# A single-core diffusion trunk with a 64-expert layer: a shorter routing chain, expert numbers written before the round table, the final sums moved into the last expert step, and two buffers for the split down weights

## The reference, cut to what matters

```python
h = h + g1 * mix
n2 = rmsnorm(h, lp['norm2_g']) * (1 + sc2) + sh2
h = h + g2 * moe(n2)
y = rmsnorm(h, final_norm_g)

def moe(x, lp):
    s = sigmoid(x @ w_router)                  # 64 experts in 8 groups of 8
    sel = s + b_router
    grp_score = top_k(sel by group, 2).sum(-1)
    gmask = the best 4 groups
    eidx = top 8 of where(emask, sel, NEG_BIG)
    w = s[eidx] / sum(s[eidx]) * 2.5
    y = sum over the 8 experts of w * (silu(x @ w_gate) * (x @ w_up)) @ w_down     # each 1024 -> 256 -> 1024
    return y + shared expert(x)
```

## Time and profile before

| what | value |
| --- | --- |
| median of 3 runs (lowest to highest) | 1113.5 us (1106.01 to 1113.51) |
| the profiled execution: own time, span | 1105.11 us, 1103.3 us |
| busy share of TensorE, its weight load, VectorE, ScalarE, GpSimd | 95%, 64%, 48%, 32%, 15% |
| granted TensorE clock, mean | 0.989 |
| DMA | 306.62 MB, mean 278 GB/s over the span |
| the chain that ended last, by engine | PE 60%, DVE 2%, issue 1%, ACT 1% |

### The profile page before, as it was taken

One profiled execution on the slowest core, in us unless ns is written; L12 is line 12 of the kernel. 1 busy time (PEld: TensorE's weight loads), 2 busy tenths in 40 slices (PEclk: granted clock), 3 DMA queues, 4 the chain that ended last, 5 costly groups with the idle time before them and its releaser, 6 DMA issues.

```text
span 1103.3 us, 15100 instructions
## 1 busy us (share of the span) xinstructions
PE 1046.7 (95%) x4876; PEld 702.0 (64%) x4876; DVE 531.1 (48%) x1110; ACT 355.2 (32%) x476; POOL 166.0 (15%) x142
## 2 busy tenths in 40 slices
PE   4999999999899999999998999999999999999975
PEld 2489888788788897874645455555555555454532
DVE  2233544355698956944633434433344334333358
ACT  3333544326444445501322222222222222222101
POOL 0020232000000000000015222322322212111100
PEclk9999999999999999999999999999999999999998
DMA  9999777346555332740249999999999999999692
GB/s 354 395 293 356 114 117 106 136 175 213 202 185 184 116 117 96 240 160 0 97 195 409 383 405 399 416 412 398 415 415 417 410 404 418 416 408 383 243 405 109
DMA packets 88529, 306.62 MB, mean 278 GB/s; under 512 B 13398, under 2 KB 17750, under 8 KB 66464
## 3 DMA queue, kind: packets, MB, share of 16 engines
q1 hardware_dynamic: 68896, 270.63, 62.2%
q0 software_dynamic: 12256, 26.80, 10.5%
q10 hardware_dynamic: 7328, 8.55, 2.2%
HBM read 285.31 MB, written 36.85 MB: 292 GB/s over the span
## 4 chain that ended last, share of the span: by engine, by line
PE 60%; DVE 2%; issue 1%; ACT 1%; DVEq 0%
PE PS L2045 17%; PE PS L2047 8%; PE PS L2070 4%; PE PS L1944 4%; PE PS L2031 3%; PE PS L1691 3%; PE PS L2060 3%; PE PS L2062 2%; PE PS L2061 2%; PE PS L2002 1%; PE PS L2119 1%; PE PS L2086 1%; PE PS L1932 1%; PE PS L1933 1%; PE PS L1934 1%
## 5 line engine op out<-in xcount | busy, mean ns | idle before, releaser
L1098 POOL DMA_INDIRECT y_parts<-bigB,IDX x38 | 72.3, 1902 | 323.8 <-DVE bigB L1628 314.7
L2045 PE MATMUL PS<-bigB 128*128 128x512 f32 x224 | 102.3, 600 | 0.0
L1745 PE MATMUL PS<-bigB_r 128*128 128x384 f32 x288 | 98.6, 342 | 1.3 <-ACT bigB L790 1.3
L2047 PE MATMUL PS<-bigA,bigB 128*64 128x512 f32 x208 | 94.7, 598 | 3.3 <-issue 3.3
L1747 PE MATMUL PS<-bigB_r,bigA_r 128*128 128x384 f32 x288 | 96.5, 335 | 0.0
L1746 PE MATMUL PS<-nT_r,bigB_r 128*128 128x384 f32 x288 | 96.3, 334 | 0.0
L2048 PE MATMUL PS<-bigB 128*64 128x512 f32 x208 | 94.8, 598 | 0.0
L2045 PE MATMUL PS<-bigA,bigB 128*128 128x512 f32 x208 | 94.6, 597 | 0.0
L1628 DVE TENSOR_SCALAR bigB<-PS,bigD 128x1024 f32<-128x1024 f32 x40 | 51.3, 1284 | 89.2 <-PE PS L2062 55.0
L1237 DVE TENSOR_TENSOR bigA_r<-bigA,bigB_r 128x2048 fp32r<-128x2048 f32 x18 | 41.3, 2292 | 97.5 <-ACT bigB_r L816 97.5
L1594 DVE TENSOR_TENSOR bigB<-bigB,PS 128x256 f32<-128x256 f32 x40 | 16.9, 422 | 134.3 <-ACT bigB L989 134.3
(11 more groups left out here) (372 smaller groups left out, 2127.2 us busy)
## 6 DMA issues: line engine op xcount, KB each, us to landing
bigA<-in_w_in SPq DMA_DIRECT2D x17, 2048.0 KB, 11.0
bigB<-in_w_gate SPq DMA_DIRECT2D x27, 1024.0 KB, 11.0
bigB<-in_w_up SPq DMA_DIRECT2D x27, 1024.0 KB, 18.9
bigB<-in_w_down SPq DMA_DIRECT2D x27, 1024.0 KB, 19.0
bigA<-in_w_gate SPq DMA_DIRECT2D x26, 1024.0 KB, 8.2
bigA<-in_w_up SPq DMA_DIRECT2D x26, 1024.0 KB, 16.6
bigA<-in_w_down SPq DMA_DIRECT2D x26, 1024.0 KB, 19.2
bigA<-in_w_ada SPq DMA_DIRECT2D x8, 2048.0 KB, 10.0
```

Of the source, the lines that this page charges most:

```text
L1098: pool.indirect_dma_start(y_parts, bass.IndirectOffsetOnAxis(ap=IDX[:, p, 1:2], axis=0), YS[:, p % 2, :], None, bounds_check=T * TOPK - 1, ...
L1745: mm(out, wh, nh, start=(k == 0), stop=False)
L2045: last = mm(PS[:, 2 + b, :], XT[:, b, k, :], GU_W[s][:, :, k, :], start=first, stop=stop)
L2047: mm(PS[0:HALF, 2 + b, :], XT[:, b, k, 0:HALF], GU_W[2][:, :, k, :], start=first, stop=stop)
```

## The change

It has four parts. **Routing:** the comparison of all pairs of groups is replaced by max8, match_replace and not_equal on the 8 group scores, the mask is made by one min, seven links are taken away by reordering operations that do not depend on each other, `mask_ready` is given before the weights, and the stages are in another order; the modulation of the third tile is shared between VectorE (k 0 to 3) and ScalarE (k 4 to 7), and its router product waits for one k at a time. **Numbers ahead of the table:** a new stage `row` makes the row of expert numbers before `table_t`, and SP starts its loads on it. **End inside the last step:** the final sums of VectorE and TensorE stand in the `Else` of each step (the branch of the last unit), one-hots and the first adds before the last `weigh`. **Two buffers:** `DNH` becomes a pair; `down_high` and `down_low` of a unit move one step ahead.

```diff
-          ("norm2", 2), ("rows", 0), ("route", 0), ("route", 1), ("norm_t", 2), ("rows", 1), ("sh_up", 0, 0, 2),
-          ("route", 2), ("router",), ("rows", 2), ("sh_up", 0, 2, 8), ("sh_silu", 0), ("sh_up", 1, 0, 3), ("counts",),
-          ("sh_up", 1, 3, 8), ("sh_silu", 1), ("sh_hid", 0), ("sh_hid", 1), ("sh_up", 2, 0, 3), ("table_t",),
-          ("sh_up", 2, 3, 5), ("table",), ("sh_up", 2, 5, 8), ("sh_silu", 2), ("index", 0), ("sh_down", 0), ("sh_hid", 2),
-          ("index", 1), ("sh_down", 1), ("index", 2), ("sh_down", 2), ("index", 3)]
+          ("norm2", 2), ("route", 0), ("route", 1), ("sh_up", 0, 0, 1), ("norm_t", 2), ("route", 2), ("router",),
+          ("rows", 0), ("sh_up", 0, 1, 4), ("rows", 1), ("sh_up", 0, 4, 7), ("counts",), ("rows", 2),
+          ("sh_up", 0, 7, 8), ("sh_silu", 0), ("sh_up", 1, 0, 4), ("row",), ("table_t",), ("sh_up", 1, 4, 5), ("sh_hid", 0),
+          ("table",), ("sh_up", 1, 5, 8), ("sh_silu", 1), ("index", 0), ("sh_hid", 1), ("index", 1), ("sh_up", 2, 0, 8),
+          ("sh_silu", 2), ("sh_down", 0), ("index", 2), ("sh_down", 1), ("sh_hid", 2), ("sh_down", 2), ("index", 3)]
...
-        DNH = cut(bigC_r, 0, (2, D))
+        DNH = [cut(bigC_r, 0, (2, D)), cut(bigD_r, 0, (2, D))]
...
-            units = unit_count(sp)
             sp.wait_ge(n2_out, 48)
+            sp.wait_ge(row_done, 1)
             for r, q in ((BIG0, 0), (BIG0 + 1, 1), (1, 3)):
...
+            act.wait_ge(sh_added, NT - 1)
+            down_high(1, 0)
             def step(i, p):
                 act.wait_ge(gu_ready, i)
-                if p % 3 < 2:
-                    down_high(pas * 4 + (p // 3 + 1), i, p % 3)
                 with act.If(i + 2 <= units):
                     take_xt(i + 1, p % 2)
                 act.wait_ge(ht_ready, i)
...
                 with act.If(i + 1 <= units):
+                    if (p + 1) % 3 < 2:
+                        down_high(pas * 4 + ((p + 1) // 3 + 1), (p + 1) % 3)
                     act.wait_ge(hid_done, i)
                     silu(i, (1 + p) % 2)
...
+            def last_sums():
+                dve.wait_ge(sh_added, NT)
+                one_row(0, 1, 1)
+                one_row(0, 2, 0)
+                one_row(0, 2, 1)
+                residual(0)
+                two_rows(1, 2)
+                one_row(1, 3, 0)
+                one_row(1, 3, 1)
+                final_norm(0)
+                residual(1)
+                m = 2
+                two_rows(m, 0)
+                one_row(m, 1, 0)
+                one_row(m, 1, 1)
+                link(nc.vector.tensor_tensor(ACC, ACC, gate(m), ALU.mult))
+                link(nc.vector.tensor_tensor(XH[:, m, :], XH[:, m, :], ACC, ALU.add))
+                final_norm(1)
+                dve.wait_ge(part_ready, m + 1)
+                link(nc.vector.tensor_tensor(two(ACC), PS[:, TAIL_BANK[m]:TAIL_BANK[m] + 2, :], two(gate(m)), ALU.mult))
+                nc.vector.tensor_tensor(XH[:, m, :], XH[:, m, :], ACC, ALU.add).then_inc(h2_done, 1)
+                dve.wait_ge(h2_done, m + 1)
+                final_norm(m)
...
             def step(i, p):
                 u = 1 + p + AHEAD
                 with dve.If(i + 1 <= units):
                     one_hots(pas * 8 + u // 3 * 2, u % 3, u % 2)
-                    down_low(p)
                     take_index(i + AHEAD, u % BODY, u % 3)
                     hidden_low(i, p)
+                    if (p + 1) % 3 < 2:
+                        down_low(pas * (BODY // 3 * 2) + ((p + 1) // 3 * 2 + (p + 1) % 3 + 1), (p + 1) % 3)
                     dve.wait_ge(ht_ready, i)
                     hidden(i, (1 + p) % 2)
+                    nc.vector.tensor_copy(TOKF[:, p % 2:p % 2 + 1], IDX[:, p, 0:1])
+                    weigh(i, p)
                 with dve.Else():
-                    down_low(p)
                     hidden_low(i, p)
+                    link(nc.vector.tensor_copy(TOKF[:, p % 2:p % 2 + 1], IDX[:, p, 0:1]))
+                    dve.wait_ge(ys_done, i)
+                    for b in range(2):
+                        for m in range(NT):
+                            ins = nc.vector.tensor_scalar(OHT[:, b, m, :], kc(K_R128), TOKF[:, b:b + 1], float(-P * m),
+                                                          ALU.subtract, ALU.is_equal)
+                    ins.then_inc(oht_done, 1)
+                    dve.wait_ge(xg_t, i)
+                    two_rows(0, 0)
+                    one_row(0, 1, 0)
+                    weigh(i, p)
+                    last_sums()
...
+                elif st == "row":
+                    pe.wait_ge(tab_ready, 1)
+                    mm(PS[0:1, 1, 0:RTAB], NCNT, ident, start=True, stop=True)
+                    mm(PS[0:1, 1, RTAB:2 * RTAB], RC[:, 0:1], ident, start=True, stop=True).then_inc(pr_ready, 1)
...
+            def last_sums(i):
+                pe.wait_ge(oht_done, 1)
+                pe.wait_ge(ys_done, i + 1)
+                kept_rows(0, True, False)
+                loaded_rows(0, 3, False, True).then_inc(part_ready, 1)
+                kept_rows(1, True, False)
+                loaded_rows(1, 0, False, False)
+                loaded_rows(1, 1, False, True).then_inc(part_ready, 1)
+                kept_rows(2, True, False)
+                loaded_rows(2, 2, False, False)
+                loaded_rows(2, 3, False, True).then_inc(part_ready, 1)
...
                     gate_up(i, turn, 1 + p, range(4, KD))
+                    finish_unit(i, p)
                 with pe.Else():
                     hidden_t(i, p)
-                pe.wait_ge(ht_done, i)
-                pe.wait_ge(ys_done, i)
-                down(pas * 4 + (p // 3 + 1), p)
+                    finish_unit(i, p)
+                    last_sums(i)
```

262 lines of the change are left out of this document (127 added, 135 removed).

## The result

The changed kernel takes 1153.77 us (median of 4 runs, 1147.83 to 1155.68) against 1109.97 us before (1106.01 to 1113.51): ratio 1.0387, interval 1.0325 to 1.0448. The forecast was 1115 us, its range ended at 1129. The profiled execution's span is 1151.9 us, 48.6 us more than before.

A forecast was written before the change was run, and what follows sets the result against it. TensorE's queue bounds routing, TensorE and DMA are both full in the loop, VectorE's sums bound the end. Terms 0.4 + 1 + 4 - 3.5 - 0.3 = +1.6 us on 1113.5 gave 1115 us; range 1101 to 1129.

The forecast's parts named there:

- the skipping of 8 leftover steps: End of the kernel: the skip now stands behind VectorE's last operation, 4 to 5 us against 3.1, +1 us.
- slower rival: Loop code outgrows the instruction store; fetches at three returns and the end, some +10 us, 1125 us; chance 0.20.
- Routing: Before the loop: earlier table and loads worth nothing, TensorE's gaps exposed by the new order, +0.4 us.
- Head of the loop: First step: VectorE's down_low goes before the one-hots and can be held by GpSimd's addition, +1 us.
- Two buffers: Loop from about 830 us: down weights must land earlier, so TensorE waits for the hidden products, +4 us.
- Last unit: Before the last down products: no down_low ahead, and fewer products at the lower clock, -3.5 us.
- End in the last step: Final sums inside the last step: -1.3 us for VectorE's sums, +1 for the skip, taken as -0.3 us.

The follow-up runs named there:

- e9: The kernel before with 13 copies a step on VectorE that never run, under a condition only the data decide: 1133.15 us, ratio 1.0185.
- e10: The kernel before with 39 products a step on TensorE that never run, under a condition only the data decide: 1166.18 us, ratio 1.0502.
- e16: The kernel before with nested conditions and VectorE's one-hots made one step ahead: 1103.3 us, ratio 0.9942.
- e8: The kernel before with the two buffers for the down weights alone, routing and end as before: 1115.3 us, ratio 1.0053.
- e7: The changed kernel with everything of the end behind the loop, one-hots, first adds and weighing included: 1121.43 us, ratio 1.0099 to the kernel before.
- e17: The changed kernel with everything of the end behind the loop, nested conditions and one-hots one step ahead: 1111.42 us, ratio 1.0003 to the kernel before.
- e12: The kernel before with nested conditions and the changed kernel's order of the last sums, behind the loop: 1115.09 us, ratio 1.0032.
- e11: The kernel before with the twelve steps' conditions nested, so one test leaves all leftover steps: 1105.69 us, ratio 0.9972.
- e13: The kernel before with 5 never executed copies a step on VectorE, compiled loop body 345 instructions: 1131.33 us, one run.
- e15: The kernel before with 12 never executed products a step on TensorE, compiled loop body 1953 instructions: 1132.67 us, one run.
- e5: The kernel before with 14 copies a step on VectorE behind a condition known ahead of the run to be false: 1109.0 us, ratio 0.9981.
- e6: The kernel before with 48 products a step on TensorE behind a condition known ahead of the run to be false: 1110.68 us, ratio 0.9998.

## Why the prediction was wrong

**The forecast's choice and the price of a rival.** The step that failed is the term for the end, "+1 us" for "the skipping of 8 leftover steps", together with what the sum left out: it has no term for the returns. The runs showed +15.3 us behind the last VectorE operation and +23.2 us at the three returns in their place, 38.5 of the 48.6 us. The forecast's whole sum was +1.6 us. The prediction had this as its slower rival: "Code size 0.20", "2 us a fetch", "+16 with all of it, some +10 with part covered": the mechanism was named, with its places (three returns, the skip at the end) and its tell-tales (packets after 730 us, a stall each twelve units, several us behind VectorE's last operation), and all of them came. Two things failed in it.

First the chance. I had counted TensorE's instructions a step (90 to 250), and the earlier trace rows showed that the old body was never drawn late. Nothing in the profile spoke against the rival, and e9 and e10 show that code which never runs is enough. It should have been the forecast. VectorE's body I had not counted at all, and gave it a price only at the end; it went from 273 to 1109 instructions, and in e9 441 cost 1.9 per cent.

Second the size. The 2 us were the difference of two walks over code that was resident (1.78 and 4.21 us); no row that I used held a fetch, so it was no measure for one. VectorE's was longer mainly because TensorE's skips lay over its last products. Measured are 5.2 to 5.8 us of stall at a return for TensorE, and 1.3 to 2.8 us more, mostly for products at the lower clock: 23.2 us instead of 6. At the end I had up to 10 us for the fetches; the walk behind the sums takes 18 us from VectorE's last operation on, 28 from TensorE's, and adds 15.3. Together 38.5 us instead of the 16 that I had called all of it.

The Trainium skill (Runtime: NRT & Kernel Launch, section "Instruction fetch mechanics") says that fetching ahead is purely sequential and that a taken branch outside the window forces a fetch before the engine can go on. The runs agree with the second in kind, most plainly in e10's skips of 2.8 to 6.1 us; the first they neither show nor deny. They disagree in the number by which a reader would judge what is safe: 345 of 512 and 1953 of 2048 instructions were already too many. The section's sentence that a long kernel needn't fit holds for straight code only; here each return, and in e10 each skipped step, was a branch out of what was there.

**Routing (+0.4, ends -1 and +3).** Held: 1.0002 alone. In the profiled executions it was +2.1 to +2.6 us at unit 1, inside the ends. The first load was issued at 554.73 us, as forecast, and was worth nothing.

```profile
554.73 0.36 SPq L663 DMA_DIRECT2D bigB<-in_w_gate  x1
```

**Head of the loop (+1, 0 to +3).** Outside its range in the profile (+5.2 us): a longer stall (3.3 us, 1.08 before) because two VectorE operations are slow instead of one, and some 3 us behind it, which I had left out: the next eight products took 6.36 us, 3.68 before, and the granted clock from 604 to 612 us was 0.60.

```profile
604.39 0.80 PE L1739 MATMUL PS<-bigD_r,bigC_r 128*128 128x8 f32 x3 [3.32 <-DVE bigD_r L1148]
```

Against the median of before it is worth less, because most executions of before pay the same (seven of eleven above, e16 for the cure). The Trainium skill (SBUF — State Buffer, section "SBUF: two separate sides") calls the two engines' shared port an exclusive lock for a whole instruction. The 2.50 us for an operation of 0.34 us in e8 agree: it has two SBUF inputs, began while GpSimd's addition was under way and ended 0.2 us behind it. The 2.31 us row that the prediction called in agreement is a cast with one input and does not show the rule as it was given there.

**Two buffers (+4, ends -3.3 and +7).** Right in size: e8 loses 5.4 us in the loop, with the clock and the old waits' gain in it. Right in the cause, the landing of the down weights, but not in the path: I had named the hidden transposes and the products of TensorE, and in e8, e7 and the changed kernel most of it is paid at the index products, because VectorE's one-hots stand behind the late `hidden` and `weigh`. Only in e17, with the one-hots hoisted, the hidden transposes wait, 5.3 us. ScalarE waits for the landing well before 830 us (in e7 from 716 us on), up to 6.3 us in e7 and 7.8 us in e17; TensorE pays from about 860 us on.

**Last unit (-3.5, ends -2 and -4).** The stall before the last L2060 (now L2109) fell from 3.59 to 1.38 us and the products behind it run 0.23 us apart, as forecast; from hidden transposes to the last `weigh` are 6.08 us, 8.73 before: -2.7. In e8 it is -3.7, but there TensorE's walk then stood bare for 3.20 us, its first eight products of the sums ran at the lower clock (6.47 us, 3.69 before), and VectorE waited 2.3 us longer for them: most of the gain went again.

**End in the last step (-0.3, ends -4 and +4).** VectorE's own part from the last `weigh` on took 37.2 us to its last operation, 39.1 before: -1.9, and the first wait, 3.4 us by my list, came out as 3.71. What stood behind it was the walk, outside both ends: here the +1 us for the skip failed.

**The forecast's own sum without length.** No run shows it clean. My +1.6 us would be 1.0014. e7, with short bodies, has the end behind the loop and measures 1.0099. e17 takes the head away as well and measures 1.0003, but it also has nested conditions and the hoisted one-hots, which help the kernel before too (e16, 0.9942): against e16 it is 0.6% slower, and e12 against e11 shows as much for the order of the sums behind the loop. e8 alone gives 1.0053, some 6 us, where my terms for it (+1 head, +4 loop, -3.5 last unit) came to +1.5; in its profile they are +5.3, +5.4 and -3.7, with 2.4 us lost again in the sums. So apart from length the head was the term most out of size, and how much of it the timed runs feel stays open, since most executions of before pay it too.

## What to carry to other kernels

Before code is put into each step of a written-out loop, count the compiled body of each engine and compare it with a body that is known to stay resident, not with the store's nominal size. Look at the instruction queues' packets by stretch: none in the loop means that it fits. Code that is only skipped still counts, and each jump to code that is not there cost TensorE 3 to 5 us with the DMA nearly empty and 5 to 6 with it full. So parts that run once belong behind the loop, and the way out of an unrolled loop should be one jump, empty passes included (that last was not tried). A stall of TensorE is to be priced with the lower clock behind it, here some 2 us on top of 5 to 6.

## What the runs showed of the hardware that I had not expected

- The way out is dearer than the returns, because it holds many fetches: 39.84 us of TensorE for eight skips over some 270 instructions each and a return to the head (e10), 19.33 us of VectorE for eight skips over 37 each and a return (e9), against 1.78 and 4.21 us with the short steps.
- One fetch behind a branch took TensorE 2.8 to 2.9 us at a DMA share of 0.06 and 5.5 to 6.1 us at 1.00 (e10).
- VectorE no longer keeps a body of 345 instructions, TensorE none of 1953 (e13, e15).
- Code under a condition that can be decided ahead of the run is removed (e5, e6); under one that data decide it stays, and costs 1.9% and 5% though it never runs (e9, e10).
- Unit 2 behind the unchanged head falls into two groups, up to 1.6 us and 3.3 to 4.8 us late, by how VectorE's one-hots meet GpSimd's additions. One profiled execution shows only one of them.
